# A hybrid decoder layer on one core: narrower stationary operands in the level products and the last delta level, and query squares by transposes and row sums

## What is computed

```python
# HGRN2, one chunk
decay = exp(where(causal, G[t] - G[s], -inf))
A = einsum('bhtd,bhtsd,bhsd->bhts', q, decay, k)
o = einsum('bhts,bhsv->bhtv', A, v) + einsum('bhtd,bhdv->bhtv', q * exp(G), S)
# Gated DeltaNet, one chunk
gq = gq * rsqrt(sum(gq * gq, -1) + EPS) * GDN_DK ** -0.5
A = beta * einsum('bhtd,bhsd->bhts', k, k) * dec_strict
sol = triangular_solve(eye + A, rhs, lower=True)
```

## Time and profile before

| | |
|---|---|
| median of 3 runs | 728.11 us (727.39 to 728.21) |
| profiled execution | 727.87 us, of which its span is 726.2 us |
| busy | PE 706.3, PEld 678.3, DVE 436.0, POOL 351.9, ACT 304.3 us |
| granted TensorE clock, mean | 0.998 |
| transfers | 44.93 MB, mean 62 GB/s |

### The profile page before, as it was taken

How to read it: one execution, slowest core, us unless ns; L and a number is a source line. 1 busy time by engine, 2 the same in 40 slices (tenths; PEclk the granted TensorE clock), 3 DMA queues, 4 the chain that set the end, 5 groups by cost and what they waited for, 6 DMA issues and landing times. The chain is left out here.

```text
span 726.2 us, 13528 instructions
## 1 busy us (share of the span) xinstructions
PE 706.3 (97%) x4858; PEld 678.3 (93%) x4858; DVE 436.0 (60%) x1018; ACT 304.3 (42%) x800; POOL 351.9 (48%) x471
## 2 busy tenths in 40 slices
PE   7999999999999999999999999999999999999995
PEld 7799999999999999999999999999999998888884
DVE  6845356279882472598934634989436257776257
ACT  6644431635544315445444154445442352232333
POOL 5782332257562422376714232767342557756333
PEclk9999999999999999999999999999999999999999
DMA  8355332221213317450639141202244306221004
GB/s 265 35 65 84 29 34 57 50 29 31 36 33 61 53 42 64 21 39 17 40 51 71 40 69 25 35 9 48 51 67 152 86 32 209 68 64 52 30 36 195
DMA packets 63989, 44.93 MB, mean 62 GB/s; under 512 B 17438, under 2 KB 59044, under 8 KB 63924
## 3 DMA queue, kind: packets, MB, share of 16 engines
q1 hardware_dynamic: 63924, 44.07, 33.7%
HBM read 35.82 MB, written 7.65 MB: 60 GB/s over the span
## 5 line engine op out<-in xcount | busy, mean ns | idle before, releaser
L258 PE MATMUL proj<-uTh,w_high 128*128 128x352 f32 (+4 forms) x768 | 261.6, 341 | 2.4 <-PEq L1742 2.4
L258 PE MATMUL proj<-uTh,w_low 128*128 128x352 f32 (+4 forms) x768 | 246.0, 320 | 0.0
L258 PE MATMUL proj<-uTl,w_high 128*128 128x352 f32 (+4 forms) x768 | 245.5, 320 | 0.0
L258 PEld LDWEIGHTS proj<-uTh,w_high 128*128 128x128 f32 x768 | 145.3, 189 | 3.3 <-issue 3.1
L258 PEld LDWEIGHTS proj<-uTl,w_high 128*128 128x128 f32 x768 | 145.3, 189 | 0.0
L258 PEld LDWEIGHTS proj<-uTh,w_low 128*128 128x128 f32 x768 | 144.4, 188 | 0.0
L276 POOL TENSOR_TENSOR w_low<-w_raw,w_high 128x256 fp32r<-128x256 f32 (+1 forms) x54 | 71.7, 1328 | 84.0 <-ACT w_high L268 36.6
L1242 POOL TENSOR_TENSOR f_suffix<-f_suffix,f_prefix 128x192 f32<-128x192 f32 x84 | 55.5, 661 | 27.7 <-DVE f_prefix L1458 21.2
L1662 PEld LDWEIGHTS mix<-level_x 128*128 128x128 f32 x448 | 60.7, 191 | 3.4 <-issue 1.2
L1662 PE MATMUL mix<-level_x 128*128 128x64 f32 x448 | 59.8, 266 | 0.0
L1505 DVE SCALAR_TENSOR_TENSOR conv_out<-conv_in,hg_taps,conv_out 128x352 f32<-128x352 f32 (+2 forms) x81 | 51.7, 638 | 0.5
(11 more groups left out here) (308 smaller groups left out, 1397.0 us busy)
## 6 DMA issues: line engine op xcount, KB each, us to landing
w_raw<-in_w_in SPq DMA_DIRECT2D x32, 512.0 KB, 8.3
x_tile<-in_x SPq DMA_DIRECT2D x8, 512.0 KB, 6.7
w_raw<-y_scratch SPq DMA_DIRECT2D x8, 384.0 KB, 4.4
decay<-gamma_scratch SPq DMA_DIRECT2D x4, 576.0 KB, 3.7
landing<-in_w_out SPq DMA_DIRECT2D x4, 512.0 KB, 8.0
landing<-in_x SPq DMA_DIRECT2D x3, 512.0 KB, 6.4
out_y<-landing SPq DMA_DIRECT2D x3, 512.0 KB, 2.6
y_scratch<-gd_y SPq DMA_DIRECT2D x6, 192.0 KB, 1.8
```

The source lines that it names most:

```text
L258: last = pe.matmul(acc[:, 0:tw], w[j % 2][:, k, :], u[:, k, t0:t0 + tw], start=(k == 0 and i == 0), stop=(k == KT - 1 and i == 2))
```

## The change

It does four things.

1. Level products: only `keys = max(128 - b, 66)` columns of `level_x` are loaded: 127, 126, 124, 120, 112, 96 and 66 for the seven levels. The moving operand stays at 64 columns. The merge takes as many partitions (64 at the seventh level).
2. Last delta level: Z is made the other way round, with the first 66 columns of Y as stationary and columns 64 to 127 of `M` as moving operand. ACT copies 66 of each 128 columns of Y, and DVE copies the block of 64 partitions by 64 columns per chunk without a mask.
3. Query squares: TensorE transposes the queries of a group (three transposes) where it multiplied the squares by a column of ones. ACT squares the three transposed chunks out of PSUM with a sum along the row (`measure_q`, in stage A3), in place of one square of the group in stage A1; the wait for `qs` of the group before and the semaphore `q_squared` go.
4. DVE no longer adds epsilon; POOL does it for all nine chunks (`rsqrt`) ahead of the power.

```diff
--- before.py
+++ after.py
@@ -67,6 +67,7 @@
 BASE = 4
 BLK = 1 << BASE
 BLKS = P // BLK
+HALF = P // 2 + 2
 ROWS = BLKS * NC
 
 
@@ -1472,10 +1473,11 @@
                                             ).then_inc(bank_free(plan, ("gram", g, 0)), 1)
                         return
                     b = 1 << (m - 1)
-                    shape = [P, n, P // (2 * b), b]
-                    src = src[:, first(g) // 2:GW // 2].rearrange("p (c n b) -> p c n b", c=n, b=b)
-                    msk = halves(mask_st[:, m, :], b)[:, :, 1, :].unsqueeze(1).broadcast_to(shape)
-                    acc = acc.rearrange("p c (n two b) -> p c n two b", two=2, b=b)[:, :, :, 1, :]
+                    keys = P - b
+                    shape = [keys, n, P // (2 * b), b]
+                    src = src[0:keys, first(g) // 2:GW // 2].rearrange("p (c n b) -> p c n b", c=n, b=b)
+                    msk = halves(mask_st[0:keys, m, :], b)[:, :, 1, :].unsqueeze(1).broadcast_to(shape)
+                    acc = acc[0:keys].rearrange("p c (n two b) -> p c n two b", two=2, b=b)[:, :, :, 1, :]
                     dve.copy_predicated(acc, msk, src).then_inc(bank_free(plan, ("gram", g, m)), 1)
 
                 def update_state(g, i):
@@ -1659,7 +1661,8 @@
                                                  start=True, stop=True)
                             else:
                                 both = X[(LEVELS * g + m - 1) % 2][:, chunk(i)]
-                                last = pe.matmul(ap[:, i * P // 2:(i + 1) * P // 2], both,
+                                keys = max(P - (1 << (m - 1)), HALF)
+                                last = pe.matmul(ap[0:keys, i * P // 2:(i + 1) * P // 2], both[:, 0:keys],
                                                  halves(both, 1 << (m - 1))[:, :, 1, :], start=True, stop=True)
                         last.then_inc(done, 1)
                         project(("gram", g, m))
@@ -1741,7 +1744,7 @@
         plan = Bank(names)
         with nc.Block() as block:
             par = sem("gd_par")
-            q_squared, rq_done = sem("q_squared"), sem("rq_done")
+            rq_done = sem("rq_done")
             ssq, rstd_s, kd_done = sem("gd_ssq"), sem("gd_rstd"), sem("gd_kd_done")
             blk_in, blk_step, blk_solved, blk_turned = (sem(n) for n in ("blk_in", "blk_step", "blk_solved", "blk_turned"))
             blk_weighed, blk_cut, blk_mout, n_set, m_set = (
@@ -1864,8 +1867,7 @@
 
 
                 freed(pool, plan, ("qs", NG - 1))
-                pool.tensor_tensor(rr[:, 1, :], ss[:, 1, :], neg_half[:, 0:1].broadcast_to([P, NC]), ALU.pow
-                                   ).then_inc(rq_done, 1)
+                rsqrt(pool, rr[:, 1, :], ss[:, 1, :], EPS * P, eps_added, NG + 1).then_inc(rq_done, 1)
 
                 for key in order:
                     if key == ("A1", 2):
@@ -1894,12 +1896,18 @@
                         last = act.activation(sq[0][:, i * P:(i + 1) * P], src[:, i * P:(i + 1) * P], ACT.Square,
                                               accum_out=ss[:, 0, g * GC + i:g * GC + i + 1])
                     last.then_inc(ssq, 1)
-                    if g:
-                        full(act, plan, ("qs", g - 1))
-                    act.activation(sq[1][:, :], xq[:, g * GW:(g + 1) * GW], ACT.Square,
-                                   scale=float(P) ** 0.5).then_inc(q_squared, 1)
                     act.copy(vtok_c[:, g * GW:(g + 1) * GW], full(act, plan, ("tv", g))[:, 0:GW]
                              ).then_inc(bank_free(plan, ("tv", g)), 1)
+                def measure_q(g):
+                    src = full(act, plan, ("qs", g))
+                    if g:
+                        freed(act, plan, ("qs", g - 1))
+                    for i in range(GC):
+                        last = act.activation(sq[1][:, i * P:(i + 1) * P], src[:, i * P:(i + 1) * P], ACT.Square,
+                                              scale=float(P) ** 0.5, accum_out=ss[:, 1, g * GC + i:g * GC + i + 1])
+                    last.then_inc(bank_free(plan, ("qs", g)), 1)
 
                 def turned(g):
                     act.copy(kT[:, g * GW:(g + 1) * GW], full(act, plan, ("tkn", g))[:, 0:GW]
@@ -1910,6 +1918,8 @@
                         measure(g)
                     elif s == "A2":
                         turned(g)
+                    else:
+                        measure_q(g)
                     if (s, g) == ("A2", 0):
                         split_high(act, 1)
                     take_hg(act, parts[(s, g)])
@@ -1919,7 +1929,10 @@
                     for g in range(NG):
                         lo = since(g) * P
                         gs = slice(g * GW + lo, (g + 1) * GW)
-                        act.copy(Y[:, gs], full(act, plan, ("Y", i, g))[:, lo:GW]).then_inc(bank_free(plan, ("Y", i, g)), 1)
+                        src, dst = full(act, plan, ("Y", i, g))[:, lo:GW], Y[:, gs]
+                        if i == LEVELS - 1:
+                            src, dst = (t.rearrange("p (c t) -> p c t", t=P)[:, :, 0:HALF] for t in (src, dst))
+                        act.copy(dst, src).then_inc(bank_free(plan, ("Y", i, g)), 1)
                     if more:
                         decay_exp(act, i - BASE, dec_sub, dec_exp)
                     take_hg(act, parts[("B1", i)])
@@ -1955,9 +1968,6 @@
                 def scores(g):
                     gs = slice(g * GW, (g + 1) * GW)
                     dec = DT[:, gs]
-                    dve.tensor_scalar(ss[:, 1, g * GC:(g + 1) * GC], full(dve, plan, ("qs", g))[:, 0:GC], EPS * P, None,
-                                      ALU.add).then_inc(bank_free(plan, ("qs", g)), 1)
 
                     kk_ = full(dve, plan, ("kk", g))
                     for i in range(GC):
@@ -2055,9 +2065,14 @@
                         lo = since(g)
                         gs = slice(g * GW + lo * P, (g + 1) * GW)
                         part3 = lambda t: t.rearrange("p (c t) -> p c t", c=GC - lo)
-                        src = part3(full(dve, plan, ("Z", i, g))[:, lo * P:GW])
-                        dst, msk = (N, mask_ts[:, min(i, LEVELS - 2) - BASE, :]) if i < LEVELS - 1 else (M, mask_st[:, LEVELS, :])
-                        dve.copy_predicated(part3(dst[:, gs]), msk.unsqueeze(1).broadcast_to([P, GC - lo, P]), src
+                        src = full(dve, plan, ("Z", i, g))
+                        if i < LEVELS - 1:
+                            msk = mask_ts[:, i - BASE, :].unsqueeze(1).broadcast_to([P, GC - lo, P])
+                            dve.copy_predicated(part3(N[:, gs]), msk, part3(src[:, lo * P:GW])
+                                                ).then_inc(bank_free(plan, ("Z", i, g)), 1)
+                        else:
+                            dve.tensor_copy(part3(M[0:P // 2, gs])[:, :, P // 2:P],
+                                            part3(src[0:P // 2, lo * P // 2:GW // 2])
                                             ).then_inc(bank_free(plan, ("Z", i, g)), 1)
                     if more:
                         decay_keep(dve, i - BASE, dec_exp)
@@ -2090,13 +2105,7 @@
                         three(("tv", g), g, full_c(xv, g))
                     elif s == "A2":
                         three(("tkn", g), g, part_c(kn), wait=("tk", g))
-                        ap, done = take(pe, plan, ("qs", g))
-                        pe.wait_ge(q_squared, g + 1)
-                        for i in range(GC):
-                            last = pe.matmul(ap[:, i:i + 1], sq[1][:, i * P:(i + 1) * P], tri[:, P - 1:P],
-                                             start=True, stop=True)
-                        last.then_inc(done, 1)
+                        three(("qs", g), g, full_c(xq, g))
                     else:
                         three(("kk", g), g, full_c(kT, g), full_c(kT, g), wait=("tkn", g))
                         three(("qk", g), g, full_c(kT, g), full_c(xq, g), lo=live(g)[0])
@@ -2114,8 +2123,16 @@
                             pe.wait_ge(m_set, g + 1)
                         if i > BASE:
                             freed(pe, plan, ("TM", i - 1, g))
-                        l, rt = (M, Y) if i < LEVELS - 1 else (Y, M)
-                        three(("Z", i, g), g, full_c(l, g), full_c(rt, g), wait=("Y", i, g), lo=since(g))
+                        if i < LEVELS - 1:
+                            three(("Z", i, g), g, full_c(M, g), full_c(Y, g), wait=("Y", i, g), lo=since(g))
+                            continue
+                        ap, done = take(pe, plan, ("Z", i, g))
+                        freed(pe, plan, ("Y", i, g))
+                        for k in range(since(g), GC):
+                            c0 = (g * GC + k) * P
+                            last = pe.matmul(ap[0:HALF, k * P // 2:(k + 1) * P // 2], Y[:, c0:c0 + HALF],
+                                             M[:, c0 + P // 2:c0 + P], start=True, stop=True)
+                        last.then_inc(done, 1)
                     project(pe, parts[("B2", i)])
```

## The result

The changed kernel takes **716.12 us** (median of 4 runs, 715.70 to 716.41) beside 728.06 us for the kernel before on the same chip: a ratio of 0.9834, 95% interval 0.9819 to 0.9849, 11.9 us less. The forecast was 12.4 us less.

A forecast was written before the change was run, and what follows sets the result against it. TensorE, busy 97% of the span, was taken as the bound, its float32 products spaced by their 128-column loads. Level products 4.4, last delta level 3.0, query squares 4.1 and ACT's wait 0.9 sum to 12.4 us: 715.7 us, range 713.5 to 719.3.

The forecast's parts named there:

- The price of a column: TensorE's float32 weight loads in a stream: each stationary column left out saves 0.83 ns.
- 16-column gate load: Gate loads, 95 ns long against 191 for 128 columns: 0.86 ns a column, bounding the gain from above.
- (a): Narrower loads take the same time; only the query part is left, 723.1 us; chance 0.08.
- (b): Load columns count in steps of 32, so 127 to 112 save nothing: 719.2 us; chance 0.06.
- Last delta level: Z loads in phase_gd: 15 a head save 49.5 ns each, 3.0 us over four heads.
- The limit of 65 ns: How fast short load and multiply can follow each other, from small transposes: 8 steps of 65 ns.
- Query squares: Query sums in phase_gd: three transposes replace six loads, 4.1 us, plus 0.9 us from ACT's removed wait.
- Rival (d): A query transpose costs its row's length in a stream, losing 1.9 us instead of winning 4.1: 721.7 us; chance 0.01.
- Level products: Level loads in phase_hg: 52 x 102 ns = 5.3 us, 0.9 given back in heads 0 to 2, net 4.4 us.
- The 0.3 of the first group: First group of phase_hg, heads 0 to 2: TensorE waits longer for DVE, giving back 0.9 us over three heads.
- Rival (c): DVE and POOL take back all level gain in heads 0 to 2; 1.3 of 4.4 us stay, 718.8; chance 0.08.
- Rival (e): Narrow loads no longer slip under the multiply in front; all 512 level and delta loads pay 0.08 us: 764; chance 0.04.

The follow-up runs named there:

- the wait alone: Kernel before with a second buffer for the squared queries, so ACT waits for the sums of two groups back instead of one: 727.34 us, ratio 0.9989.
- the convolution cut: DVE's convolution steps limited to 32 columns, rest left out: on the kernel before 725.45 us (0.9962), on the changed kernel 712.54 us (0.9787).

## Why the prediction held

**What bounds the kernel** was read rightly. TensorE lost 12.1 us of busy time and the span 12.0; the new waits that appeared are of 0.2 us each.

**The price of a column** (0.83 ns) measured 0.82, and columns count singly: 110, 86 and 60 ns at 127, 96 and 66 in the rows above, against 111, 84 and 60 to 65 forecast. The 16-column gate load had been a fair witness though of another type. Rivals (a), one price at all widths, and (b), steps of 32, are both refuted by these rows; the first by 724.16 us for the levels alone as well.

**Last delta level**: 3.0 forecast, 3.12 measured alone. I had taken 62 ns a load, between the 59 of the count by column and the 65 of the small transposes, and it was 60. The limit of 65 ns does not hold for these products: at 64 columns the loads come 55 to 58 ns apart.

**Query squares** with ACT's wait: 4.1 + 0.9 = 5.0 forecast, 4.98 measured. The transposes are 12 x 0.34 = 4.1 by their rows; the wait alone is worth 0.7 in its own kernel, so some 0.2 us of the match has no term of its own. Rival (d), a transpose at its row's length, is refuted: three take 0.32 us. The figure of about 275 ns for a 128x128 transpose that the Trainium skill gives (TensorE: Matmul & The Clock Gate, Part 4: PE-mode transpose) is near the length of one such row here, 0.27 us, and not what one costs in a stream, 0.11; the granted clock was 1.00 around them.

**Level products**: 4.4 forecast, 3.83 alone and 4.24 in the whole change. This is the term that was mis-sized. The gross gain was right (head 3: 1.3 forecast; the level groups, each from its first multiply to the product behind, became 1.36 us shorter, and the phase lost 1.50, of which 0.14 is not accounted for). What heads 0 to 2 give back was forecast as 0.3 us each and was 1.50 - 0.91 = 0.6 beside head 3 in the change (0.4 if measured by the 1.33 counted), 0.7 alone. The 0.3 of the first group was right in size, though part of it waits at the state's products (L839) and not at `level_x`. What I missed is the third group: I had looked for room in the later groups at one place only, the `level_x` of the first level, and not at the transposes of `gd_on`, which had no room at all and cost another 0.2 us a head. Against the 1.0 forecast for each of heads 0 to 2 it came to 0.91, 0.3 us short in all; head 3 gained 0.2 more than forecast, which is not accounted for and made up for half of that, by luck. With the convolution cut the wait of the third group is gone in all three phases, and that of the first in two. Rival (c), all of the gain given back, had the direction right, and was to take 1.3 us a phase where 0.6 to 0.7 went.

**Rival (e)**, the slower case, did not happen at 66 columns: the first load of a group still starts with the multiply in front. But it is real two columns further down, and its price is 0.28 us for a change of width in both directions, not 0.08 us for each load. What I held against it, gate multiplies with 16 stationary columns that follow each other without a gap, was no evidence, since inside a stream the 64-column loads have no gap either. The evidence was at the two ends of the gates' stream, where nothing is lost; and even that, with other operands, does not carry over to 64 columns of these.

## What to carry to other kernels

When float32 products are spaced by their loads (here up to 128 moving columns), cut stationary columns, not moving ones: each was worth 0.82 ns a load, two loads a product, down to 66 columns and 60 ns, the narrowest that paid here. Ask of every triangular or block product which rows of the result are read at all, and whether a sum by a column of ones (two loads) can be a transpose (one load) with the sum left to an idle engine. Then look through the stages where another engine has no pause: there only a part arrives (0.9 us in place of 1.5 for the whole phase). And look at every wait behind them, not only the nearest: the second loss stood two groups later, at a load that had come exactly on time.

## What the hardware showed that I had not expected

A load of 64 stationary columns behind a multiply with 128 did not start under that multiply, and a 128-column load behind the group of 64 was late too: 0.94 us against 0.66 around one group, 3.2 us in the whole time, for two columns less. At 66 nothing of it is seen, and nothing at the 16 columns of the gates' products either. No width between 64 and 66 was run, nor another one below 64 with these operands, so where the edge lies and what it hangs on is open. The time is lost on each entry and exit: the stream of 16 loads of 64 columns in `phase_gd` pays about as much (0.26 us) as a group of 4 or 6.
